# First feed-forward of a conditioned encoder layer in pairs of gated tiles, with seven block products for the down product and a conditioning ring of three

## What is computed

```python
def swiglu(h, wg, wu, wd):
    return (jax.nn.silu(h @ wg) * (h @ wu)) @ wd

mod = jax.nn.silu(c) @ ada_w[l] + ada_b[l]
sh1, sc1, g1, sh2, sc2, g2, sh3, sc3, g3 = jnp.split(mod, N_MOD, axis=-1)
h = modulate(rmsnorm(x, ffn1_norm[l]), sh1, sc1)
x = x + 0.5 * g1[:, None, :] * swiglu(h, ffn1_wg[l], ffn1_wu[l], ffn1_wd[l])
...                                    # token mixing, with sh2, sc2, g2
h = modulate(rmsnorm(x, ffn2_norm[l]), sh3, sc3)
x = x + 0.5 * g3[:, None, :] * swiglu(h, ffn2_wg[l], ffn2_wu[l], ffn2_wd[l])
```

## Time and profile before

| | us |
|---|---|
| median of 3 runs | 3033.53 (3032.97 to 3038.99) |
| profiled execution | 3033.41 |
| its span | 3031.6 |
| first feed-forward, half 0, half 1 | 522.80, 520.40 |
| second feed-forward, first and second half | 503.40, 518.80 |

### The profile page before, as it was taken

One profiled execution on the slowest core, in us unless ns is written; L12 is line 12 of the kernel. 1 busy time (PEld: TensorE's weight loads), 2 busy tenths in 40 slices (PEclk: granted clock), 3 DMA queues, 4 the chain that ended last, 5 costly groups with the idle time before them and its releaser, 6 DMA issues.

```text
span 3031.6 us, 49322 instructions
## 1 busy us (share of the span) xinstructions
PE 2915.9 (96%) x16297; PEld 2687.0 (89%) x16297; DVE 1684.7 (56%) x2862; ACT 1501.3 (50%) x2515; POOL 2065.9 (68%) x1046
## 2 busy tenths in 40 slices
PE   7899999999999999997989999999999998999998
PEld 3899999999999988885656667989999998999998
DVE  5766664676666656886543332275443466544545
ACT  7433333533333366766767775444444455444444
POOL 1766666776666663334547666678898887989894
PEclk9999999999999999998999999999999999999999
DMA  8233332133333234557313225441212242221224
GB/s 279 77 101 100 104 107 80 56 91 111 100 100 104 77 114 145 137 147 177 103 51 91 71 78 151 121 138 61 84 55 83 65 134 92 62 84 55 83 70 160
DMA packets 368360, 310.76 MB, mean 103 GB/s; under 512 B 22012, under 2 KB 324463, under 8 KB 368239
## 3 DMA queue, kind: packets, MB, share of 16 engines
q1 hardware_dynamic: 365102, 307.62, 33.8%
q10 hardware_dynamic: 3136, 1.57, 0.2%
HBM read 257.00 MB, written 52.13 MB: 102 GB/s over the span
## 4 chain that ended last, share of the span: by engine, by line
PE 63%; POOL 16%; issue 9%; DVE 4%; DMA 3%; ACT 3%; SPq 2%; ACTq 0%; POOLq 0%; DVEq 0%
PE PS L3135 9%; PE PS L3137 9%; PE PS L3136 9%; POOL W_lo L2520 8%; PE PS L444 7%; PE PS L445 7%; PE PS L446 7%; POOL quart L2533 4%; DMA quart<-in_ffn_wu 2%; PE PS L1533 1%; PE PS L1478 1%; PE PS L1535 1%; PE PS L1534 1%; POOL XT_r L1770 1%; PE PS L3189 1%
## 5 line engine op out<-in xcount | busy, mean ns | idle before, releaser
L3135 PE MATMUL PS<-SL,W_hi 128*128 128x384 f32 x2112 | 715.5, 339 | 34.0 <-POOL W_lo L2520 16.8
L3136 PE MATMUL PS<-SL,W_hi 128*128 128x384 f32 x2112 | 709.6, 336 | 0.0
L3137 PE MATMUL PS<-SL,W_lo 128*128 128x384 f32 x2112 | 709.4, 336 | 0.0
L1980 DVE SCALAR_TENSOR_TENSOR XT<-PS,mod,XT 128x384 f32<-128x384 f32 (+1 forms) x880 | 440.1, 530 | 278.9 <-PE PS L446 200.8
L2440 POOL TENSOR_TENSOR W_lo<-quart,W_hi 128x1024 fp32r<-128x1024 f32 x132 | 326.5, 2482 | 316.3 <-ACT W_hi L2434 316.3
L2520 POOL TENSOR_TENSOR W_lo<-quart,W_hi 128x1024 fp32r<-128x1024 f32 x192 | 469.7, 2467 | 55.2 <-ACT W_hi L2515 55.1
L3135 PEld LDWEIGHTS PS<-SL,W_hi 128*128 128x128 f32 x2112 | 399.3, 189 | 43.7 <-POOL W_lo L2520 20.5
L1770 POOL TENSOR_TENSOR XT_r<-XT,XT_r 128x512 fp32r<-128x512 f32 x224 | 286.8, 1286 | 178.6 <-ACT XT_r L1622 178.2
L3136 PEld LDWEIGHTS PS<-SL,W_hi 128*128 128x128 f32 x2112 | 399.3, 189 | 1.0 <-issue 1.0
L3137 PEld LDWEIGHTS PS<-SL,W_lo 128*128 128x128 f32 x2112 | 399.5, 189 | 0.0
L2515 ACT ACTIVATE W_hi<-quart 128x1024 fp32r<-128x1024 f32 x192 | 200.6, 1059 | 277.8 <-PE PS L3191 124.0
(11 more groups left out here) (337 smaller groups left out, 6860.1 us busy)
## 6 DMA issues: line engine op xcount, KB each, us to landing
quart<-in_ffn_wg SPq DMA_DIRECT2D x176, 256.0 KB, 3.1
quart<-in_ffn_wu SPq DMA_DIRECT2D x176, 256.0 KB, 3.5
down<-in_ffn_wd SPq DMA_DIRECT2D x48, 512.0 KB, 3.3
quart<-in_ffn_wd SPq DMA_DIRECT2D x80, 256.0 KB, 2.9
raw<-in_w_out SPq DMA_DIRECT2D x30, 512.0 KB, 4.3
ada_w_sb<-in_ada_w SPq DMA_DIRECT2D x6, 2048.0 KB, 17.8
SLf<-in_ada_w SPq DMA_DIRECT2D x64, 192.0 KB, 2.7
ada_r<-in_ada_w SPq DMA_DIRECT2D x64, 192.0 KB, 3.0
```

The costliest lines, as they stand in the source:

```text
L1980: mm = dve.scalar_tensor_tensor(out=xt, in0=PS[:, bank, a - c * NB:b - c * NB], scalar=hgate[:, g, m, s:s + 1], in1=xt, op0=ALU.mult, op1= ...
L3135: pe.matmul(out, w_hi, m_hi, start=j in PRODUCT_OPENS and kp == 0, stop=False, skip_group_check=True)
L3136: pe.matmul(out, w_hi, m_lo, start=False, stop=False, skip_group_check=True)
L3137: mm = pe.matmul(out, w_lo, m_hi, start=False, stop=kp == 3, skip_group_check=True)
```

## The change

The first feed-forward takes the spots of the second (`ffn_*` functions with f = 0 or 1 in place of `st_*` and `ffn2_*`): five pairs of GA, GB, DN and one SO for each half, 5 x 504 + 264 = 2784 matmuls a pass in place of 11 x 264 = 2904. In all four passes, ACT's plain copies of two of the gated values (B22 and T2) go: DVE writes the gated value to its SBUF home itself (`mult_dve` with `exact`; value 3 is multiplied twice, once for each place), and the differences T1, T3, T2 are formed in that order ahead of their low parts. The home of T4 is a row of the parked half. Parking and unparking are done in the first feed-forward as well; the first part comes back after 16 of the 28 outputs of the last DN, the second at SO.

The conditioning's 16 turns lie in GA and GB of the pairs 1 to 4 of each half, with a ring of three slots:

```diff
-AR = 4
+AR = 3
...
+        def ada_load(sp, S, k):
+            sp.wait_ge(ada_chain, S.ada_chain(max(k - AR + 1, 0)))
...
             def spot(S):
-                if S.first:
-                    park(S.h)
-                N = S.ahead()
+                N, last = S.ahead(), S.kind == DN and isinstance(S.p, int) and S.p == PAIRS - 1
+                for k in range(6) if S.ada() else ():
+                    ada_load(sp, S, k)
                 spot_load(sp, N, A11Q, sum_ready, S.sums(4))
+                for k in range(6, KD) if S.ada() else ():
+                    ada_load(sp, S, k)
                 spot_load(sp, N, A21Q, unit_ready, S.unit(5))
                 spot_load(sp, N, A22Q, unit_ready, S.unit(6))
+                if last:
+                    unpark(sp, S.h, 0)
                 spot_load(sp, N, A12Q, unit_ready, S.unit(7))
+                if S.first:
+                    park(sp, S.h)
...
+                for k in range(before) if S.ada() else ():
+                    ada_sum(dve, S, k)
                 add_dve(dve, S, 0)
...
+                if S.ada():
+                    for k in range(before, KD):
+                        ada_sum(dve, S, k)
+                    ada_fold(dve, S)
+                    ada_mods(dve, S)
                 add_dve(dve, S, 1)
                 add_dve(dve, S, 2)
...
+            if n == 3 and S.kind != SO and not exact:
+                dve.wait_ge(st_prod, S.prod(3, True))
+            dve.tensor_tensor(exact_home(n) if exact else up, silu_home(S, n), up, ALU.mult).then_inc(st_prod, 1)
...
             def gate_up(S):
                 for j in range(PN):
                     spot_product(pe, S, j)
                     if S.first and S.h == 2 and j in (T2, T3):
                         sums_pe(pe, 2, NWC - 1, j - T2)
+                    if S.kind == SO and S.h == 1 and j in (B11, B21, T1, T2):
+                        sums_pe(pe, 1, 0, ((B11, B21, T1, T2).index(j),))
+                    if S.ada() and j == T3:
+                        ada_reduce(pe, S)
```

More of the change, by code:

```diff
@@ L2148, in op_lo_dve @@
                .then_inc(op_ready, 1)
[L2150 to L2163, removed]
@@ L2186, in build @@
[L2186 to L2244, removed]
-                if self.kind in (GA, GB):
-                    return Spot(self.kind + 1, self.h, self.p, self.back)
-                if self.kind == DN:
-                    return Spot(GA, self.h, self.p, self.back - 1)
-                return Spot(GA, 3, 0)
@@ new lines, in ffn_loads @@
+        def ffn_loads(sp, f):
+            S0 = Spot(GA, 2 * f, 0)
+            if f == 0:
+                ada_block_load(sp, 4)
+                sp.wait_ge(x_turned, NT + 2)
+                sp.wait_ge(x_summed, NT)
+                spot_load(sp, S0, A11Q)
+                ada_block_load(sp, 5)
+                spot_load(sp, S0, A12Q)
+            else:
+                spot_load(sp, S0, A11Q)
+                sp.wait_ge(op_x, OPX0 + 2 * XN + RAW_NO[2][B22])
+                spot_load(sp, S0, A12Q)
+                sp.wait_ge(wo_ready, NWC * KD)
@@ new lines, in wait_used, with spot_hi @@
+        def wait_used(eng, S, u):
+            if S.kind == DN:
+                eng.wait_ge(d_steps, S.down(4 * u + 4))
+            else:
+                eng.wait_ge(st_steps, S.step(2 * u + 2 if u < PN else SN))
+        def spot_hi(act, S, u):
+            if u >= PN:
+                act.wait_ge(down_landed[u - PN], S.down_row(16))
+            elif u in (0, 1, 5):
+                act.wait_ge(quart_landed[UNIT_FROM[u]], S.quart(32))
+            else:
+                act.wait_ge(sum_ready, S.sums({2: 1, 3: 3, 4: 2, 6: 4}[u]))
+            if u >= WS:
+                wait_used(act, S, u - WS)
+            elif S.first and S.h == 0:
@@ L2547, in spot @@
                     pool.wait_ge(unit_ready, S.unit(PN + 1))
-                if S.kind != SO or S.h == 2:
+                if S.ahead() is not None:
                     spot_sum(pool, S.ahead(), 0)
                     spot_lo(pool, S.ahead(), 0)
-            spot_lo(pool, Spot(GA, 2, 0), 0)
-            spots(pool, spot, spot, spot)
+            S0 = Spot(GA, 2 * f, 0)
+            spot_lo(pool, S0, 0)
+            if f == 0:
+                for no in range(3):
+                    spot_sum(pool, S0, no)
+                spot_lo(pool, S0, 1)
+            spots(pool, f, spot, spot, spot)
         BX, BY, BZ, BV = 0, 2, 4, 6
@@ L2606, in keep_act @@
             act.wait_ge(st_steps, S.step(product_step((B11, T2, T3)[which], role)))
-            if which == 0:
-                act.wait_ge(part_added, S.added(role - 3))
-            if which == 1:
-                act.wait_ge(part_added, S.added(role - 1))
+            if which < 2 and S.first and S.h > 0:
+                act.wait_ge(part_added, S.added(role + (-3, -1)[which]))
+            if which < 2 and not S.first:
+                act.wait_ge(t_made, S.made(-1 + which))
             if which == 2:
@@ L2661, in gate_up @@
             def gate_up(S):
-                N = S.ahead()
+                N, turned = S.ahead(), S.first and S.h % 2
                 if S.kind == GB:
                     tail(S)
-                elif S.first and S.h == 3:
+                elif turned:
                     spot_hi(act, S, 1)
@@ L2674, in gate_up @@
                 spot_hi(act, S, 3)
-                if S.first and S.h == 3:
-                    op_hi_act(act, 3, T3)
+                if S.first and S.h == 0:
+                    for j in (T4, B22):
+                        op_hi_act(act, 0, j)
+                if turned:
+                    op_hi_act(act, S.h, T3)
                 spot_hi(act, S, 4)
@@ L2684, in gate_up @@
                 keep_act(act, S, 3)
-                if S.first and S.h == 3:
+                if S.first and S.h != 2:
                     silu_act(act, S, 0)
@@ L3110, in st_product @@
[L3110 to L3127 removed]
+            spots(dve, f, gate_up, down, single)
@@ L3248, in single @@
                 gate_up(S)
-                st_down(pe, 1, S.round(), S.h, False)
-            spots(pe, gate_up, down, single)
+                single_down(pe, S)
+            spots(pe, f, gate_up, down, single)
+            if f == 0:
+                sums_pe(pe, 1, 1)
+                pe.wait_ge(st_acc, Spot(SO, 1).acc(2 * KD))
         @block.sync
```

963 lines of the change are left out of this document (357 added, 606 removed).

## The result

The changed kernel takes 3053.62 us (median of 5 runs, 3051.49 to 3062.69) against 3035.16 us for the kernel before beside it (3032.97 to 3038.99): ratio 1.0069, 95% interval 1.005 to 1.0088. It is slower by 0.7%. The forecast was 3019 us, faster, with a range of 3002 to 3044; the time lies above the range and on the other side.

What follows compares the result with a forecast made beforehand. PE, busy for 96% of the span, was taken to bound the kernel. From 3033.4 us profiled, -41.7 + 21.2 + 1.3 + 5.9 - 1 = -14.3 us gave 3019 us, with a range of 3002 to 3044.

Steps and rivals of the forecast that it cites:

- Matmuls: First feed-forward on PE: 240 fewer matmuls at 0.1736 us each, all on the path, -41.7 us.
- The conditioning turn: PE waits at ada_reduce for DVE's fold, 1.45 us in GA and 1.2 in GB; +21.2 us over eight pairs.
- t0: Time from a gated tile's start to SP's issue of the next tile's A11Q; taken as 13.1 us, ends 12.4 and 14.1.
- The clock: Rival: half-speed matmuls after each of 16 PE waits, 27 us on top, 3046 us; chance 0.06.
- Parking and unparking: DMA transfers in the first feed-forward, costed at nothing beyond the +5.9 us at the turn of halves.
- -1 for the last unpark coming sooner: Part of the dropped copies term: fewer small PE waits and a sooner last unpark, -1 us, ends -2 and +4.
- turn of halves: First feed-forward: SO and the first pair replace two rounds, 147.49 us from SO's start to the second pair's; +5.9 us.
- Dropped copies: ACT loses two copies in each GA-GB pair, DVE gains one multiplication: -1 us, ends -2 and +4.
- Entries: First feed-forward's first tiles: POOL starts late, one wait of up to 3.2 us possible at the second tile; +1.3 us.
- The sum without the waits: Forecast total with no PE waits in the conditioning turns: -35.5 us, so 2998 us.
- the break-even at 2.2 us: PE wait per gated tile at which the conditioning turns' waits cancel the gain: 35.5 / 16 = 2.2 us.

Runs made afterwards that it cites:

- both mends: Changed kernel with all eight conditioning loads ahead of A11Q and the first part of the unparking behind A12Q: 3001.01 us, ratio 0.989 to the kernel before.
- the loads later still: Changed kernel with the last two conditioning loads of a turn moved behind the A21Q quarter too: 3106.41 us, ratio 1.025 to the kernel before.
- one load behind: Changed kernel with only the eighth conditioning load behind A11Q, the other seven ahead of it: 3018.82 us, ratio 0.9956 to the kernel before.
- the last experiment: Kernel with both mends, ACT's dropped copies of B22 and T2 put back in all four passes: 3018.84 us, ratio 0.9949 to the kernel before.

## Why the prediction was wrong, point by point

- *Matmuls, -41.7.* Right: 240 go, and with both mends the first feed-forward's windows show it, less what follows.
- *The conditioning turn, +21.2.* This is the step that failed, in its size and in what was left out of it: it cost 31.8 us of waits by the profile and 10.8 of clock, 42.6 in all. The mechanism and the place were right, and t0 in 14 of the 16 turns: A11Q went out at 12.8 to 13.1 us, where 13.1 was taken. The waits alone are 10.6 over the term, for two reasons. The transfer was mis-sized: 3.3 us was taken from between the earlier trace rows, and it was 3.9 in GA and 3.6 to 3.9 in GB (medians of the seventh and the eighth), nearly that behind four quarter loads. And in the first turn of each half POOL had not slid forward yet: A11Q went out at 15.0 and 14.3 us, and PE waited 3.4 and 3.3 us.
- *The clock, a rival at 0.06.* It was dismissed for all waits or none, and it happened for 7 of 16: 10.8 us, on top of waits that the forecast already held. The row that I had set against it, the mean clock of 0.988, says little: these 7 runs of matmuls at half speed took it only to 0.983, and the 16 of the kernel with the loads later still to 0.976. The Trainium skill ("TensorE: Matmul & The Clock Gate", Part 1) says that the array's clock is gated by its recent activity; the runs with longer waits agree, 16 of 16 with the loads later still, none in the kernel with one load behind.
- *Parking and unparking, costed at nothing beyond the turn, and -1 for the last unpark coming sooner.* Wrong in sign. The unpark ahead of A12Q delayed the later DMA of that quarter by 4.7 us (8.0 in place of 3.3) and made PE wait in the single rounds: about 4 us at the turn of halves, where SO's start to the second pair's took 705.00 - 552.97 = 152.03 us in place of the forecast 147.5 (148.0 with both mends), and 5.0 and 3.6 us in the second feed-forward's two. I had costed the two conditioning loads on SP's queue and not the 1.5 MB ahead of a quarter. (The last two numbers are worked out from the matmul starts: the time of the single round's 168 gated matmuls, after less before.)
- *Dropped copies.* Right in sign: the pairs of the second feed-forward got shorter by 3.4 us in all, above the bound of 2 that I had given. In the new order they would have cost far more, 18 us, as the last experiment shows.
- *Entries, +1.3.* The first tiles of the first feed-forward came out 0.7 us better than the rounds before. The stage ahead of them ended 2.0 us later (78.7 in place of 76.7); in the other kernels it ended between 77.4 and 79.8, and the cause stays open.

In sum, against the forecast: 10.6 (waits) + 10.8 (clock) + 4.5 (turn of halves) + 6.2 (second feed-forward, 8.6 - 3.4 where -1 was taken) - 2.0 (entry) + 2.0 (start) = 32.1 of the 34.5 us by which the span missed. Of the rest, 1.6 are about 0.1 us in each turn that the idle time by the profile doesn't count, and 0.5 is one wait for W_lo in the first conditioned tile.

The sum without the waits was 2998 us in the prediction; the kernel without waits and with the unpark mended takes 3001. The frame held, then, and the break-even at 2.2 us of wait in a tile as well: the wait was 2.0 with 0.7 of clock on top, on the wrong side of it. The forecast stood 0.9 us in a tile from that point, and two unknown prices of that size lay between.

What stays open is why the two loads take 3.9 us and not 3.3. The kernel with one load behind A11Q answers it in part: its load goes out 1.2 us behind A11Q and 1.2 us ahead of the next quarter, as the seventh does in the changed kernel, and lands in 3.2 to 3.4 us, so some 0.4 to 0.6 us come with the eighth load beside it. Why one load takes longer there than ahead of A11Q, where it was 2.4, was not tried.

## What to carry to other kernels

Before a waiting instruction is put inside a stretch that runs on one engine without idle time, follow its last input back to the queue that issues it, and count everything ahead of it in that queue: here two loads of 192 KB behind a 512 KB quarter ate the gain of 240 matmuls, and putting them ahead, with one sum moved to match, gave 40 us back. A wait that is moved along the engine that waits isn't removed when the engine that is late has more consumers. Multiply the error of a small per-tile price by the number of tiles before choosing a sign: 0.9 us was enough in 16 tiles.

## What the runs showed of the hardware

Whether a wait of PE brings half speed behind it was not settled by its length alone. With idle times by the profile: all 16 of 3.5 us and more in the kernel with the loads later still were followed by it, none of the seven of up to 1.45 us in that with one load behind, and of the 16 between 1.2 and 3.4 us in the changed kernel seven were. In the kernel with the unparking behind A12Q one of 1.59 us was followed by it and one of 2.92 us was not. In the changed kernel one of 1.65 us was:

```profile
761.90 0.25 PE L532 MATMUL PS<-ada_part,fold 128*32 128x6 f32 x8 [1.65 <-DVE ada_part L515]
...
763.33 0.53 PE L2848 MATMUL PS<-X,W_hi 128*128 128x384 f32 x1
763.65 0.53 PE L2849 MATMUL PS<-X,W_hi 128*128 128x384 f32 x1
```

That of 2.01 us at 391.24 was not (the second matmul behind it started at 391.72, and the tile went on at full pitch). At 761.90 the slow level began 1.2 us after PE had resumed; behind the wait of 5.04 us it was there at once.
